# Dense heads of a two-layer encoder: the first half projection of a step ahead of the turned probabilities, and ScalarE's first exponential ahead of two copies

## The chip, the cores and the metric

The kernel runs on one core of one Trainium2 chip. The metric is the device time in microseconds (us); lower is better.

## The reference

The program is a trunk of two encoder layers over 16 meta tokens and 1024 real tokens, 1024 wide, in float32. Each layer projects the tokens, runs three groups of heads side by side (A: windowed attention, B: dense attention, C: a gated recurrence), projects back and normalises. The change touches group B only:

```python
def attend(q_blk):
    s = jnp.einsum('bqhcd,bkhcd->bhcqk', q_blk, k).astype(jnp.float32) * scale
    s = jnp.where(key_ok, s, NEG)
    p = jax.nn.softmax(s, axis=-1)
    a = p[:, :, 0] - lam * p[:, :, 1]
    return jnp.einsum('bhqk,bkhv->bqhv', a.astype(v.dtype), v)
```

There are four dense heads. Each has two components c of 64 wide queries and keys, and the two softmaxes are combined into one matrix `a`, which weighs values 128 wide. Queries and keys are rotated (RoPE) ahead of it, and the result is normalised and gated.

## The kernel before

The whole kernel is one hand-ordered program for five instruction streams: TensorE (PE), ScalarE (ACT), VectorE (DVE), GpSimd (POOL) and the DMA queue of SyncE. Each stream runs strictly through its own list and waits on semaphores. There is no planner at run time; the same Python lists are walked by every engine's builder, so that the counts agree.

**Tiles and steps.** Tokens lie in nine tiles (eight of 128 rows and one, the last, of 16 meta rows). Layer 0 needs all nine query tiles, layer 1 only the eight real ones. A *step* is one query tile t of one dense head g (B0 to B3). Steps run head by head, tile by tile. `b_step(l, g, t, k)` names the step k places further on.

**What a step does.** For step (g, t) the engines do the following, in `pass_b` of each engine.

- PE writes the scores of the *next* step (`scores`, L1116, 12 matmuls, two banks of PSUM per component: banks 2/3 and 4/5). It then waits for `b_comb`, DVE's combined probabilities `p0_b` of *this* step, and turns them by transposes in three groups of three tiles (`transposes(t, 0..2)`, L1272). Group 0 goes to bank 0, group 1 to bank 1, and group 2 to bank 0 again, so group 2 waits until ACT has copied group 0. Then come the products with the values (`values`, L1288, 18 matmuls with three copied groups as their input: tiles 0 to 5, then 6 to 8).
- DVE takes the maximum of the next step's scores for component 0 and for component 1 (`maximum`, L2131 and L2132, which writes `neg_max`), does low parts and rotations for the next head (`qk_lo` L2087, `qk_rope` L2073 to L2079), finishes the step before (`finish`, L2157 and L2160), and combines the next step's two exponentials (`combine`, L2141 to L2147; L2145 makes `p0_b` and raises `b_comb`).
- ACT copies the turned groups to `aT_b` (`evac_probs`, L1622), computes the next step's exponentials (`exps(after, c)`, L1610 and L1612; each waits for `b_max` of its component), copies the values (L1632) and computes the norm (L1639 to L1643).
- POOL splits weights into a high and a low part beside DVE's maxima (`beside_maximum`). SP moves rotated pieces, results and weights.

**ACT's order before**, in every step: copies of groups 0 and 1; the casts of a rotated piece if the step has one (`qk_hi_of`, L1585, for the pieces 0 and 1); the exponential of component 0; the copy of group 2; the cast of piece 2 if there is one; the exponential of component 1; `values_out`; `norm`.

**Projections inside the steps.** While one head attends, PE projects the queries and keys of the head behind it. Each projection (a feature half and a piece of 346 or 348 tokens, 24 matmuls, L944) is cut in two halves of 12 matmuls, and `b_steps(l, nx)` deals these halves out as `parts` of the steps. In layer 0 the heads B0, B1 and B2 have 2, 2, 1, 1, 1, 1, 1, 1, 2 halves, the same, and 2, 2, 2, 1, 1, 0, 0, 0, 0 over their nine steps. In layer 1 B0 and B1 have 2, 2, 2, 1, 1, 1, 1, 2 and B2 has 2, 2, 2, 2, 0, 0, 0, 0 over eight steps. B3 has none. In the very first step of B0 both halves are placed ahead of everything else on PE, and `parts` is emptied there. A projection of feature half f uses bank 7 - f. Before the change the first half of a step lies between the turned groups 1 and 2, the second between group 2 and the values.

**The last step of a head** also turns the next head's meta scores (`meta_turned` on PE, L1237 and L1241, in bank 6; `meta_out` on ACT, L1599 and L1600; `meta_bound` on DVE, which the next maximum needs). The projection in that step uses bank 6, too, and waits for `meta_out`.

The deal of halves, from `b_steps`:

```python
halves = [(nx, u, half) for u in units(l, nx, "qk") if u not in early(nx) for half in range(2)]
q, r = divmod(len(halves), n - 3 if after_next(nx) else n - 4)
ends = [(t + 1) * q + min(t + 1, r) for t in range(n)]
parts = [halves[a:b] for a, b in zip([0] + ends, ends)]
```

Of the kernel before, what the change touches and what calls it, by code (L numbers as in the profile page):

```python
# [63 lines left out]
def rows(t):  # L64
    return META if t == MT else P
# [422 lines left out]
def build(nc, x, meta, emb_ln_g, emb_ln_b, w_in, w_out, a_sink, b_lam, c_lb_logits, norm_cols,  # L488
# [3 lines left out]
    def sb(stack, name, shape, dt=F32):  # L492
        return stack.enter_context(nc.sbuf_tensor(name, shape, dt))
# [67 lines left out]
    qk = sb(sc, "qk", [P, 4, TOK])  # L561
# [115 lines left out]
    def slot_of(g):  # L677
        return (head_no(g) + 1) % 2
# [259 lines left out]
    def _(pe):  # L938
# [306 lines left out]
        def pass_b(l, g, nx):  # L1245
            def scores(step):
                if step is None:
                    return
                g, t = step
                sl = slot_of(g)  # L1250
                if t == 0:
                    pe.wait_ge(qk_lo_done, QK_PIECE[l, g, "qk", len(T_PIECES) - 1])
                m = rows(t)
                keys = [("s", l, g, t, c) for c in range(2)]
                for key in keys:
                    wait_free(pe, key)
                for i in range(2):
                    last = row_product(
                        lambda c: psum[0:m, bank(keys[c]) + i, :],
                        lambda a, c: qk_b[c * HD:(c + 1) * HD, sl, 2 * a, cols(t)],  # L1260
                        lambda b, c: qk_b[c * HD:(c + 1) * HD, sl, 2 * b + 1, i * 512:(i + 1) * 512])
                for key, ins in zip(keys, last):
                    ins.then_inc(filled[bank(key)], 1)

            def transposes(t, j):
                m = rows(t)
                key = ("aT", l, g, t, j)
                b = bank(key)
                wait_free(pe, key)
                for i in range(3):  # L1270
                    k = 3 * j + i
                    last = nc.tensor.transpose(psum[:, b, i * P:i * P + m],  # L1272
                                               p0_b[0:m, B_STEP[l, g, t] % 2, k * P:(k + 1) * P], ident[0:m, 0:m])
                last.then_inc(filled[b], 1)

            def values(t, ks=range(TILES)):
                m = rows(t)
                key = ("o", l, g, t)
                b = bank(key)
                if ks[0] == 0:  # L1280
                    if t == 0:
                        wait_read(pe, ("unit", l, g, "vg", TILES - 1))
                    wait_free(pe, key)
                for k in ks:
                    if k % 3 == 0:
                        wait_read(pe, ("aT", l, g, t, k // 3))

                    last = nc.tensor.matmul(psum[0:m, b, 0:P], aT_b[:, k, 0:m], vg_b[:, head_no(g), k, 0:P],  # L1288
                                            start=k == 0, stop=k == TILES - 1)
                if ks[-1] == TILES - 1:  # L1290
                    last.then_inc(filled[b], 1)

            if g == "B0":
                pe.wait_ge(b_pad, l + 1)
                scores((g, 0))
            for t, parts, _, _ in b_steps(l, nx):
                if (g, t) == ("B0", 0):

                    for h, x, half in parts:
                        project(l, h, "qk", x, half)  # L1300
                    parts = []
                scores(b_step(l, g, t, 1))
                if nx and t == q_tiles(l) - 1:
                    meta_turned(l, nx)
                pe.wait_ge(b_comb, B_STEP[l, g, t])
                transposes(t, 0)
                transposes(t, 1)
                if nx == B_HEADS[-1] and t == q_tiles(l) - 2:
                    meta_scores(l, nx)
                for h, x, half in parts[:1]:  # L1310
                    project(l, h, "qk", x, half)
                transposes(t, 2)
                for h, x, half in parts[1:2]:
                    project(l, h, "qk", x, half)
                values(t, range(6))
                if not nx and t >= Y_LAG:
                    transpose_y(l, t - Y_LAG)
                values(t, range(6, TILES))
                for h, x, half in parts[2:]:
                    project(l, h, "qk", x, half)  # L1320
                if after_next(nx) and t == q_tiles(l) - 2:
                    meta_scores(l, nx)
                for x in output_beside(nx, t):
                    project(l, "O", 0, x)
# [31 lines left out]
    def _(act):  # L1356
# [245 lines left out]
        def pass_b(l, g, nx):  # L1602
            def exps(step, c):
                g, t = step
                n = B_STEP[l, g, t]
                m, i = rows(t), n % 2
                act.wait_ge(b_max, B_COMP[l, g, t, c])
                b = bank(("s", l, g, t, c))
                probs = p0_b[0:m, i] if c == 0 else p1_b[0:m]
                nc.scalar.activation(probs[:, REAL * P:TOK], meta_s[0:m, slot_of(g), c, t, :], ACT.Exp, scale=SCALE,  # L1610
                                     bias=neg_max[0:m, i, c:c + 1], accum_out=row_sum[0:m, i, 2 * c + 1:2 * c + 2])
                nc.scalar.activation(probs[:, 0:REAL * P].rearrange("p (i n) -> p i n", i=2), psum[0:m, b:b + 2, :],  # L1612
                                     ACT.Exp, scale=SCALE, bias=neg_max[0:m, i, c:c + 1],
                                     accum_out=row_sum[0:m, i, 2 * c:2 * c + 1]).then_inc(released[b], 1)

            def evac_probs(t, j):
                key = ("aT", l, g, t, j)
                b, m = bank(key), rows(t)
                wait_filled(act, key)
                if b_step(l, g, t, -1) and j == 0:  # L1620
                    wait_filled(act, ("o", l, *b_step(l, g, t, -1)))
                nc.scalar.copy(aT_b[:, 3 * j:3 * j + 3, 0:m],  # L1622
                               psum[:, b, 0:3 * P].rearrange("p (k c) -> p k c", k=3)[:, :, 0:m])\
                    .then_inc(released[b], 1)

            def values_out(t):
                key = ("o", l, g, t)
                n, b = B_STEP[l, g, t], bank(key)
                wait_filled(act, key)
                if n > 2:  # L1630
                    act.wait_ge(b_y, n - 2)
                nc.scalar.copy(o_b[0:rows(t), n % 2, :], psum[0:rows(t), b, 0:P]).then_inc(released[b], 1)  # L1632

            def norm(step):
                g, t = step
                n, m = B_STEP[l, g, t], rows(t)
                wait_read(act, ("o", l, g, t))
                act.wait_ge(b_scale, n)
                then(nc.scalar.activation(b_junk[0:m, :], o_b[0:m, n % 2, :], ACT.Square,  # L1639
                                          accum_out=sumsq[0:m, t, 0:1]))  # L1640
                then(nc.scalar.activation(rstd[0:m, t, 0:1], sumsq[0:m, t, 0:1], ACT.Ln, bias=eps_rms[0:m],
                                          scale=fscale[0:m, n % 4, :]))
                nc.scalar.activation(rstd[0:m, t, 0:1], rstd[0:m, t, 0:1], ACT.Exp, scale=-0.5).then_inc(rstd_ready, 1)  # L1643

            if g == "B0":
                exps((g, 0), 0)
                exps((g, 0), 1)
            for t, _, _, before in b_steps(l, nx):
                after = b_step(l, g, t, 1)
                if nx and t == q_tiles(l) - 1:  # L1650
                    meta_out(l, nx)
                evac_probs(t, 0)
                evac_probs(t, 1)
                for j in before:
                    if j < len(T_PIECES) - 1:
                        qk_hi_of(l, nx, j)
                if after:
                    exps(after, 0)
                evac_probs(t, 2)
                for j in before:  # L1660
                    if j == len(T_PIECES) - 1:
                        qk_hi_of(l, nx, j)
                if after:
                    exps(after, 1)
                values_out(t)
                norm((g, t))
                if nx and t == q_tiles(l) - 2:
                    meta_rows_out(l, nx)
                if not nx and t >= Y_LAG:
                    hi_of_rows("y", l, t - Y_LAG)  # L1670
# [620 lines left out]
```

## Time and profile before

| | us |
|---|---|
| median of 3 runs | 1686.74 |
| lowest and highest | 1682.14, 1890.09 |
| the profiled execution | 1683.42 |
| its span | 1682.0 |
| layer 0, windows of heads B0, B1, B2 | 67.50, 72.50, 71.00 |

The profile is of one execution. The span is what its trace covers; the profiled execution's own time is 1.4 us more. In the rows, L944 is line 944 of the kernel. PE is TensorE's matmuls and PEld its weight loads. A row of a timeline gives the start in us from the start of the span, the length in us, the engine, the line, the operation with its output and inputs, the number of instructions merged into it (x12), and in brackets the idle time of the engine ahead of it with what released it. Instructions of one engine overlap in part, so times from start to start are better measures than the lengths.

### The profile page before, as it was taken

To read this page: it belongs to the slowest core of one execution; us is meant where nothing else is said; L and a number is where in the kernel's file an instruction comes from. 1 tells how busy PE (TensorE), PEld (TensorE's weight loads), DVE (VectorE), ACT (ScalarE), POOL (GpSimd) and SP (SyncE) were. 2 spreads that over 40 slices of the span, in tenths; PEclk is the share of its full clock that TensorE was granted. 3 is DMA by queue.
4 is the path that set the end of the run, shared out by engine and by line. 5 is a ranking of instruction groups with operands and counts; after the bars stand their busy time and mean duration, and the time that the engine had idled before them with its cause. 6 is when DMAs were issued, how large, how long until landed. Compare 5 with 4: busy or idle time off the path is not lost.

```text
span 1682.0 us, 38542 instructions
## 1 busy us (share of the span) xinstructions
PE 1564.1 (93%) x15296; PEld 1462.0 (87%) x15296; DVE 1072.4 (64%) x2421; ACT 874.8 (52%) x2569; POOL 408.2 (24%) x390
## 2 busy tenths in 40 slices
PE   3899999999999999789989999999999899987997
PEld 3899999999888888678989999999999789876897
DVE  7486684446557788775265866844555678787526
ACT  5444545356627676774045445452564477767504
POOL 5332321310121102020554413213103101112054
PEclk9999999999999999999999999999999999999999
DMA  7110201200120111143122102012002111114312
GB/s 280 52 52 14 65 27 37 80 30 11 39 85 17 50 26 50 37 141 109 51 76 90 52 14 65 27 36 79 30 11 72 53 26 51 51 27 146 107 65 101
DMA packets 97859, 102.32 MB, mean 61 GB/s; under 512 B 7504, under 2 KB 87744, under 8 KB 97424
## 3 DMA queue, kind: packets, MB, share of 16 engines
q1 hardware_dynamic: 96720, 98.78, 18.3%
q8 instruction: 123, 2.02, 0.5%
q10 hardware_dynamic: 960, 1.07, 0.2%
q14 instruction: 56, 0.46, 0.1%
HBM read 70.14 MB, written 21.17 MB: 54 GB/s over the span
## 4 chain that ended last, share of the span: by engine, by line
PE 59%; DVE 20%; ACT 11%; issue 4%; POOL 3%; DMA 3%; SPq 0%; ACTq 0%; DVEq 0%; POOLq 0%
PE psum L944 43%; PE psum L1288 3%; ACT p_b L1612 3%; PE psum L1272 3%; PE psum L1116 3%; DVE p_b L2145 3%; DVE row_max L2131 2%; DVE s_a L2001 2%; POOL w_lo L909 2%; ACT aT_b L1622 2%; PE psum L1013 2%; ACT pT_a L1528 1%; PE psum L991 1%; DMA qk_t<-rot 1%; ACT p_b L1610 1%
## 5 line engine op out<-in xcount | busy, mean ns | idle before, releaser
L944 PE MATMUL psum<-w_hi,hT_hi 128*128 128x256 f32 x1824 | 523.0, 287 | 9.5 <-POOL w_lo L909 8.2
L944 PE MATMUL psum<-w_hi,hT_lo 128*128 128x256 f32 x1824 | 513.1, 281 | 0.0
L944 PE MATMUL psum<-w_lo,hT_hi 128*128 128x256 f32 x1824 | 513.0, 281 | 0.0
L905 POOL CAST w_hi<-w_raw 128x512 fp32r<-128x512 f32 (+1 forms) x168 | 110.7, 659 | 1147.1 <-DMA w_raw<-in_w_in 685.9
L944 PEld LDWEIGHTS psum<-w_hi,hT_hi 128*128 128x128 f32 x1824 | 343.5, 188 | 18.3 <-POOL w_lo L909 10.1
L944 PEld LDWEIGHTS psum<-w_lo,hT_hi 128*128 128x128 f32 x1824 | 343.6, 188 | 0.0
L944 PEld LDWEIGHTS psum<-w_hi,hT_lo 128*128 128x128 f32 x1824 | 343.6, 188 | 0.0
L944 PE MATMUL psum<-hT_hi,w_hi 128*128 128x346 f32 (+1 forms) x672 | 226.0, 336 | 5.5 <-DVE hT_lo L1739 5.4
L909 POOL TENSOR_TENSOR w_lo<-w_raw,w_hi 128x512 fp32r<-128x512 f32 (+1 forms) x168 | 216.1, 1286 | 24.4 <-DVE neg_max L2132 12.5
L944 PE MATMUL psum<-hT_lo,w_hi 128*128 128x346 f32 (+1 forms) x672 | 217.8, 324 | 0.0
L944 PE MATMUL psum<-hT_hi,w_lo 128*128 128x346 f32 (+1 forms) x672 | 217.8, 324 | 0.0
L2131 DVE TENSOR_REDUCE row_max<-psum 128x1 f32<-128x1024 f32 x136 | 165.7, 1218 | 20.6 <-PE psum L1116 20.4
L1288 PE MATMUL psum<-vg_b,aT_b 128*128 128x128 f32 (+1 forms) x1224 | 155.4, 278 | 8.6 <-ACT aT_b L1622 8.4
L1288 PEld LDWEIGHTS psum<-vg_b,aT_b 128*128 128x128 f32 (+1 forms) x1224 | 142.6, 186 | 15.0 <-ACT aT_b L1622 11.8
L1612 ACT ACTIVATE p_b<-psum,neg_max 128x1024 f32<-128x1024 f32 x136 | 150.1, 1103 | 0.0
L944 PEld LDWEIGHTS psum<-hT_hi,w_hi 128*128 128x128 f32 x672 | 128.3, 191 | 7.9 <-issue 6.9
L1622 ACT COPY aT_b<-psum 128x384 f32<-128x384 f32 (+1 forms) x204 | 87.7, 463 | 88.2 <-PE psum L1272 87.0
L944 PEld LDWEIGHTS psum<-hT_hi,w_lo 128*128 128x128 f32 x672 | 128.5, 191 | 0.0
L944 PEld LDWEIGHTS psum<-hT_lo,w_hi 128*128 128x128 f32 x672 | 128.0, 191 | 0.0
L1116 PE MATMUL psum<-qk_b 64*128 64x512 f32 (+1 forms) x816 | 113.0, 408 | 13.7 <-ACT p_b L1612 13.2
L1272 PEld LDWEIGHTS psum<-ident,p_b 128*128 128x128 f32 (+1 forms) x612 | 67.2, 141 | 54.4 <-DVE p_b L2145 31.9
L1272 PE MATMUL psum<-ident,p_b 128*128 128x128 f32 (+1 forms) x612 | 92.9, 278 | 21.6 <-DVE p_b L2145 14.5
(179 smaller groups left out, 2372.8 us busy)
## 6 DMA issues: line engine op xcount, KB each, us to landing
w_raw<-in_w_in SPq DMA_DIRECT2D x72, 256.0 KB, 3.8
w_raw<-in_w_in SPq DMA_DIRECT2D x28, 512.0 KB, 4.4
h_dram<-hbuf SPq DMA_DIRECT2D x16, 512.0 KB, 2.9
w_raw<-in_w_out SPq DMA_DIRECT2D x16, 512.0 KB, 4.4
hbuf<-h_dram SPq DMA_DIRECT2D x16, 512.0 KB, 5.8
qk_b<-y_dram SPq DMA_DIRECT2D x16, 512.0 KB, 3.5
y_dram<-y_stage SPq DMA_DIRECT2D x96, 64.0 KB, 1.6
qk_t<-rot SPq DMA_DIRECT2D x56, 86.5 KB, 2.2
```

Source lines behind the costliest of these rows:

```text
L905: pool.tensor_copy(hi, raw).then_inc(w_hi_done, 1)
L909: pool.tensor_tensor(lo, raw, hi.bitcast(F32), ALU.subtract).then_inc(w_split, 1)
L944: last = nc.tensor.matmul(out_ap, lhs[a](k), rhs[b](k), start=k == 0 and a + b == 0, stop=k == KT - 1 and b == 1)
L1013: return nc.tensor.matmul(o_ap, k_sel[rs, k_at:k_at + H_ROWS], q_ap, start=True, stop=True)
L1116: last = [nc.tensor.matmul(out_of(r), q_of(a, r), k_of(b, r), start=i == 0, stop=i == 2) for r in range(2)]
L1272: last = nc.tensor.transpose(psum[:, b, i * P:i * P + m], p0_b[0:m, B_STEP[l, g, t] % 2, k * P:(k + 1) * P], ident[0:m, 0:m])
L1288: last = nc.tensor.matmul(psum[0:m, b, 0:P], aT_b[:, k, 0:m], vg_b[:, head_no(g), k, 0:P], start=k == 0, stop=k == TILES - 1)
L1612: nc.scalar.activation(probs[:, 0:REAL * P].rearrange("p (i n) -> p i n", i=2), psum[0:m, b:b + 2, :], ACT.Exp, scale=SCALE, bias=neg_max[ ...
L1622: nc.scalar.copy(aT_b[:, 3 * j:3 * j + 3, 0:m], psum[:, b, 0:3 * P].rearrange("p (k c) -> p k c", k=3)[:, :, 0:m])\
L2001: then(nc.vector.tensor_tensor_reduce(s_a[0:m, i, h, 0:w], psum[0:m, bank(key), 0:w], band_sb[0:m, band_columns(t)], 1.0, NEG, ALU.add, AL ...
L2131: then(nc.vector.tensor_reduce(row_max[0:m, i, c:c + 1], psum[0:m, b:b + 2, :], AX.XY, ALU.max))
L2145: stt(p0_b[0:m, i, 0:TOK], p1_b[0:m, :], coef[0:m, j, 0:1], p0_b[0:m, i, 0:TOK], ALU.mult, ALU.add).then_inc(b_comb, 1)
```

## The change

On PE, the first half projection of a step moves from between the turned groups 1 and 2 to ahead of the wait for `b_comb`, right behind the next step's scores (and behind `meta_turned` in a head's last step). The second half stays between group 2 and the values. On ACT, in the steps that have a half projection and a step behind them, the exponential of component 0 moves from behind the copies of groups 0 and 1 (and the casts behind them) to ahead of them. Steps without a half projection keep their order on both engines.

```diff
--- before.py
+++ after.py
@@ -1302,13 +1302,13 @@
                 scores(b_step(l, g, t, 1))
                 if nx and t == q_tiles(l) - 1:
                     meta_turned(l, nx)
+                for h, x, half in parts[:1]:
+                    project(l, h, "qk", x, half)
                 pe.wait_ge(b_comb, B_STEP[l, g, t])
                 transposes(t, 0)
                 transposes(t, 1)
                 if nx == B_HEADS[-1] and t == q_tiles(l) - 2:
                     meta_scores(l, nx)
-                for h, x, half in parts[:1]:
-                    project(l, h, "qk", x, half)
                 transposes(t, 2)
                 for h, x, half in parts[1:2]:
                     project(l, h, "qk", x, half)
@@ -1645,16 +1645,18 @@
             if g == "B0":
                 exps((g, 0), 0)
                 exps((g, 0), 1)
-            for t, _, _, before in b_steps(l, nx):
+            for t, parts, _, before in b_steps(l, nx):
                 after = b_step(l, g, t, 1)
                 if nx and t == q_tiles(l) - 1:
                     meta_out(l, nx)
+                if after and parts:
+                    exps(after, 0)
                 evac_probs(t, 0)
                 evac_probs(t, 1)
                 for j in before:
                     if j < len(T_PIECES) - 1:
                         qk_hi_of(l, nx, j)
-                if after:
+                if after and not parts:
                     exps(after, 0)
                 evac_probs(t, 2)
                 for j in before:
```

## Rows read from the trace of the kernel before

**Rows 1.** The page: busy time of each engine, and the chain by engine and line.

```profile
PE 1564.1 (93%) x15296; PEld 1462.0 (87%) x15296; DVE 1072.4 (64%) x2421; ACT 874.8 (52%) x2569; POOL 408.2 (24%) x390
...
PE 59%; DVE 20%; ACT 11%; issue 4%; POOL 3%; DMA 3%; SPq 0%; ACTq 0%; DVEq 0%; POOLq 0%
```

**Rows 2.** Windows: from-to, us, busy (instructions) of PE, PEld, DVE, ACT, POOL; clock; DMA share; GB/s.

```profile
559.40:631.90 72.50, 68.60 (x515) 60.12 (x514) 56.91 (x127) 50.75 (x152) 7.62 (x8) 1.00 0.14 38
```

**Rows 3.** Timeline of PE in one step with one half projection: start, length, group.

```profile
543.10 1.65 PE L1116 MATMUL psum<-qk_b 64*128 64x512 f32 x12
...
545.06 0.87 PE L1272 MATMUL psum<-ident,p_b 128*128 128x128 f32 x6 [0.32 <-DVE p_b L2145]
...
547.69 0.49 PE L1272 MATMUL psum<-ident,p_b 128*128 128x128 f32 x3
...
550.23 1.57 PE L1116 MATMUL psum<-qk_b 64*16 64x512 f32 x12
```

**Rows 4.** Timeline of ACT in the same step.

```profile
545.64 0.86 ACT L1622 COPY aT_b<-psum 128x384 f32<-128x384 f32 x2 [1.20 <-PE psum L1272]
...
546.44 0.31 ACT L1610 ACTIVATE p_b<-meta_s,neg_max 128x16 f32<-128x16 f32 x1
...
548.22 0.48 ACT L1622 COPY aT_b<-psum 128x384 f32<-128x384 f32 x1 [0.28 <-PE psum L1272]
...
548.59 0.31 ACT L1610 ACTIVATE p_b<-meta_s,neg_max 128x16 f32<-128x16 f32 x1
```

**Rows 5.** Timeline of DVE in the same step and at its end.

```profile
544.99 1.22 DVE L2131 TENSOR_REDUCE row_max<-psum 128x1 f32<-128x1024 f32 x1
...
550.19 0.16 DVE L2141 TENSOR_TENSOR inv_sum<-row_sum 128x2 f32<-128x2 f32 x1
...
552.13 1.21 DVE L2131 TENSOR_REDUCE row_max<-psum 16x1 f32<-16x1024 f32 x1
```

**Rows 6.** Timeline of PE in one step with two half projections.

```profile
569.00 1.65 PE L1116 MATMUL psum<-qk_b 64*128 64x512 f32 x12
...
570.58 0.87 PE L1272 MATMUL psum<-ident,p_b 128*128 128x128 f32 x6
...
573.19 0.49 PE L1272 MATMUL psum<-ident,p_b 128*128 128x128 f32 x3
...
577.52 1.65 PE L1116 MATMUL psum<-qk_b 64*128 64x512 f32 x12
```

**Rows 7.** Timelines of DVE and ACT in the same step.

```profile
570.68 1.23 DVE L2131 TENSOR_REDUCE row_max<-psum 128x1 f32<-128x1024 f32 x1 [0.91 <-PE psum L1116]
...
572.32 0.31 ACT L1610 ACTIVATE p_b<-meta_s,neg_max 128x16 f32<-128x16 f32 x1 [0.29 <-DVE neg_max L2132]
...
573.72 0.48 ACT L1622 COPY aT_b<-psum 128x384 f32<-128x384 f32 x1
```

**Rows 8.** Timeline of a step of the last head, which has no half projection.

```profile
721.56 0.87 PE L1272 MATMUL psum<-ident,p_b 128*128 128x128 f32 x6 [0.30 <-DVE p_b L2145]
...
722.14 0.86 ACT L1622 COPY aT_b<-psum 128x384 f32<-128x384 f32 x2 [1.45 <-PE psum L1272]
...
722.68 0.55 PE L1272 MATMUL psum<-ident,p_b 128*128 128x128 f32 x3 [0.24 <-ACT aT_b L1622]
```

**Rows 9.** Timelines of PE and ACT in a head's last step.

```profile
562.43 0.43 PE L944 MATMUL psum<-hT_hi,w_hi 128*128 128x348 f32 x1
...
564.54 0.35 PE L1272 MATMUL psum<-ident,p_b 16*128 16x16 f32 x3
...
566.07 0.18 ACT L1622 COPY aT_b<-psum 128x48 f32<-128x48 f32 x1
```

**Rows 10.** Timeline of ACT: the cast of a rotated piece.

```profile
588.97 0.79 ACT L1585 CAST qk_b<-qk_t 128x696 fp32r<-128x696 f32 x1
```

**Rows 11.** A long wait of PE, and the window behind it.

```profile
710.43 0.83 PE L1288 MATMUL psum<-vg_b,aT_b 128*16 128x128 f32 x6 [2.01 <-ACT aT_b L1622]
...
712.00:714.00 2.00, 2.00 (x12) 1.50 (x12) 1.79 (x5) 0.93 (x4) 0.00 (x0) 0.65 0.80 225
```

## Prediction, made before the changed kernel was run

> **What bounds the kernel now.** I read the page first, then the windows over the dense heads, then the timelines of three kinds of step. On the page the reader should see that TensorE is busy for 1564.1 us of a span of 1682.0 and carries 59% of the chain that ended last [rows 1]. So time is gained only where PE stands still, and lost wherever a new wait of PE appears. In the dense heads the window over head B1 of layer 0 shows PE busy for 68.60 of 72.50 us, at the full clock (1.00, the 2.4 GHz level) [rows 2]: about 4 us in nine steps to win there.
>
> A step with **one** half projection is a ring through three engines. Call C the moment at which DVE has combined the two probability matrices and goes on to the next maximum (544.99) [rows 5]. Then the first turned groups start on PE at C+0.07 (545.06), behind a wait of 0.32 for the combine, and the third group at C+2.70 (547.69), after the half projection [rows 3]. ACT copies that group at C+3.23 (548.22) and starts the second exponential at C+3.60 (548.59) [rows 4]. DVE reads its sum at C+5.20 (550.19) and is ready for the next maximum at C+7.14 (552.13), which is the next C [rows 5]. Scores to scores is 7.13 us (543.10 to 550.23) [rows 3]. ACT's first exponential starts at C+1.45 (546.44), released by DVE's negated maximum, and has room in front of the third copy, which sits idle for another 0.28 [rows 4].
>
> A step with **two** half projections takes 8.52 us (569.00 to 577.52), and PE has no wait in it [rows 6]; DVE waits for PE's scores, 0.91 us [rows 7]. There PE is the bound.
>
> **The steps that change.** From the planner's list: layer 0 has 22 steps, layer 1 has 19, in which a projection moves on PE (B0 without its first step, B1, and the first five or four steps of B2). Of these 41, 22 have one half and 19 have two; 4 of the 19 are a head's last step. ACT's order changes in the same 41 and in the first step of each layer's B0. No matmul, copy or DMA is added or removed: the cost is wholly one of waits. No queue of SP or POOL is reordered, and the banks of the moved half (6 and 7) are used by no turned group, so their order stays.
>
> **What is removed.** PE's wait for the combine ahead of the turned groups, 0.32 us in a single step [rows 3], none in a double one [rows 6]. From the scores' start to the turned groups' it takes 1.96 us in the single step (543.10 to 545.06) and 1.58 in the double one (569.00 to 570.58) [rows 3, 6], so at most 0.38 us is to be had 22 times: 8.4 us.
>
> **What is added, single step.** The half projection used to lie between groups 0/1 and group 2. It covered two things: ACT's copy of group 0, whose bank group 2 needs, and the first exponential. Now group 2 follows directly, and ACT has the exponential queued ahead of the copies. The exponential can't move up: it waits for the negated maximum, and DVE starts that maximum only at C. So it starts at C+1.45 as now [rows 4]. It holds ACT for 1.40 us (572.32 to 573.72) [rows 7], so copy 0 starts at C+2.85. Behind a copy, group 2 starts 0.54 us after the copy's start (722.14 to 722.68) [rows 8]: C+3.39, in place of C+2.70. From there the ring is the old one: copy 2 after 0.53, second exponential after 0.37, sum after 1.60, next maximum after 1.94 [rows 3 to 5]. The next C is 7.83 us after this one, against 7.14: **+0.69 us**. Is the projection itself late? PE's next scores start 2.54 us behind the third group [rows 3], at C+5.93; the scores take 1.58 to the next start and the half projection 2.11 (562.43 to 564.54) [rows 6, 9], so it is over at C+9.62, 1.8 us into the next ring, and with 0.58 from turning to copy (545.06 to 545.64) [rows 3, 4] the copies could start 2.4 us into it, ahead of the exponential's end at 2.85. So it is the exponential, not the projection, that decides. Queued behind it on ACT are all three copies, and PE stands at group 2 with group 2, the values and the next scores behind it.
>
> **Double step.** Count from the scores' start P. DVE's maximum starts at P+1.68 (570.68), ACT's exponential 1.45 later and copy 0 at P+4.53; group 2 follows at P+5.07. Today it starts at P+4.19 (573.19) [rows 6, 7]. PE has no wait to shrink there, so all of it counts: **+0.88 us** each. That holds for 15 double steps, and for the first single step behind each of the five runs of double ones, where PE is still the bound: 20 x 0.88 = 17.6 us. The other 17 single steps give 17 x 0.69 = 11.7 us.
>
> **A head's last step** computes the next head's scores, whose maximum is late because the meta scores come first. Now the third group starts at 564.54, with the half projection ahead of it from 562.43; the exponential ends only at 566.07, where a copy starts [rows 9]. Behind the change the two first copies start there, and group 2 between 0.3 (copies of 16 rows, layer 0) and 0.54 us later [rows 8]: at 566.4 to 566.6, or +1.8 to +2.1 us. The four steps cost 4 x 1.95 = 7.8 us. The moved half needs the bank that the meta scores leave; it starts at 562.43 in both orders, since it already waits there now [rows 9].
>
> **The two first steps of B0** get ACT's new order alone: +0.7 each as in a single step, 1.4 us. **The casts** (0.79 us, [rows 10]) of eleven of the reordered steps stood between the copies and the exponential and now stand behind both. They delay the third copy by about as much as before, but in one step (layer 0, B1, step 2) DVE has the cast's rest and a whole rotation to do behind it: some 1.6 us in all, my estimate.
>
> **Sum:** 17.6 + 11.7 + 7.8 + 1.4 + 1.6 = 40.1 us, on the profiled execution's 1683.4 (span 1682.0 and 1.4 around it): 1723.5, say **1724 us**. The median shown is 1686.74, 0.2% above the profiled execution, which lies nearer to the lowest run (1682.14); I forecast on the profiled one. No row of the kernel before shows this order of exponential and copies, so its cost has bounds on both sides: below, -8.4 us, if the copies were never late and only the waits went; above, 41 x 1.40 = 57 us, if every step paid a whole exponential. I take the ring's value because each link in it has a row.
>
> **Rivals.** *A. Only PE-bound steps pay.* If the single rings have more slack than I read, their 0.69 disappears and 28 us remain: 1712 us, within 2%. For it: DVE waits here and there. Against it: the links of the ring add up to 7.14 exactly, with no slack. *B. The clock gives way.* A wait of 2.01 us at 710.43 was followed by a window with a granted clock of 0.65, a mixture of the 1.2 and 2.4 GHz levels [rows 11]; the waits of the last steps grow to about 1.5 us. If the clock fell in each of the four, PE would lose up to half of some 4 us, 2 us each: +8, 1732 us. Against it: the 4 us that PE stands still in the nine steps of B1 leave that window at 1.00 [rows 2]. *C. Faster, on the other side.* If ACT takes the groups' copies in time, that is, if the exponential's 1.40 us were already over when group 0 is turned, only the combine wait goes: 1683.4 - 8.4 = 1675 us. It decides from the point at which the exponential starts before C+1.0 (group 0 is ready at C+2.4 in the new order); it starts at C+1.45 in the rows. *D. Nothing happens*, because the moved half only swaps one wait for another of equal length: 1683 us.
>
> The Trainium skill ("TensorE: Matmul & The Clock Gate", Part 4: PE-mode transpose) says that transposes do not count as PE activity in the way matmuls do. By that rule the new waits, which stand between turned groups, would look longer to the clock, and rival B would be likelier. The trace has turned groups beside waits in each single step and shows 1.00 in that window [rows 2], so I leave B small.
>
> **Chances.** The ring as worked out 0.77 (1724, own range 1712 to 1732, of which about 0.08 is below 2%), A 0.08, B 0.10, C 0.02, D 0.03. "Slower by over 2%" begins at about 1717 from the profiled execution; 2% is about what a measurement of this kernel can tell from no change. Slower: 0.69 + 0.10 = 0.79; same: 0.08 + 0.08 + 0.02 + 0.02 = 0.20; faster by over 2%: 0.01. The range 1706 to 1738 takes in A and B and leaves C and D out.
>
> **What would show it.** Right: in single steps PE waits about 1 us at the third group for ACT's copy, and scores to scores is 7.8; double steps take 9.4 us with a wait of 0.88 at the same place; last steps grow by about 2; the waits for the combine vanish from the steps with a half projection, and ACT's exponential starts 1.45 us behind each maximum with the copies right behind it. Wrong: if the third group starts less than 0.3 us behind the first two, or if the first exponential starts earlier than C+1.2, or if the steps of head B3, whose order is as before, change their length.

## The result, and the profile after

The changed kernel takes 1726.5 us (median of 4 runs, 1724.2 to 1728.4) against 1686.7 us for the kernel before (one of its four executions took 1890.1 us and is left out). The ratio on record is 1.0248, with a 95% interval of 1.0233 to 1.0262: slower. The two medians alone give 1.0236, which lies inside the interval. The forecast was 1724 us, slower, with a range of 1706 to 1738. The runs of before made later on other chips have medians of 1684.6 and 1683.5 us, so the difference in microseconds is nearer to 42 than to the 39.8 between the two medians. The spans of the two profiled executions say the same: 1724.3 less 1682.0 is 42.3 us.

The page of the changed kernel, busy time by engine and the chain by engine:

```profile
PE 1579.9 (92%) x15296; PEld 1467.2 (85%) x15296; DVE 1071.2 (62%) x2421; ACT 873.5 (51%) x2569; POOL 406.9 (24%) x390
...
PE 53%; DVE 22%; ACT 14%; issue 4%; POOL 3%; DMA 3%; SPq 0%; ACTq 0%; DVEq 0%; POOLq 0%
```

Beside [rows 1], PE's share of the chain fell from 59% to 53%, while DVE and ACT hold more of it. The number of instructions is the same. The window over head B1 of layer 0, with the columns of [rows 2]:

```profile
566.10:647.70 81.60, 70.83 (x515) 60.36 (x514) 56.87 (x127) 50.51 (x152) 7.53 (x8) 1.00 0.13 34
```

It was 72.50 us long and is 81.60, still at a clock of 1.00. PE's busy sum has grown a little, from 68.60 to 70.83, while the work is the same: a pipelined instruction that follows a wait shows a longer duration, and a busy sum doesn't tell work from such tails. Start-to-start times do.

What PE waited for (line waited at and releaser: us in total, times, longest), first in the kernel before,

```profile
PE psum L1272 <- DVE p_b L2145: 14.5, 35, 1.1
...
PE psum L1116 <- ACT p_b L1612: 13.2, 26, 1.2
...
PE psum L1288 <- ACT aT_b L1622: 8.4, 15, 2.0
...
PE psum L1272 <- ACT aT_b L1622: 5.3, 22, 0.2
```

then in the changed one:

```profile
PE psum L1272 <- ACT aT_b L1622: 44.8, 64, 2.4
...
PE psum L1116 <- ACT p_b L1612: 11.1, 22, 1.2
...
PE psum L1272 <- DVE p_b L2147: 7.3, 16, 1.0
...
PE psum L1288 <- ACT aT_b L1622: 6.4, 14, 1.4
```

These four lines show what the change did to PE's waits. The wait for the combined probabilities has halved, by 7.2 us. The wait for ACT's copies at the third turned group was 5.3 us in 22 short waits, and is 44.8 us in 64, up to 2.4 us long. The other two lines shrink by 2 us each. Together the four grew by 28.2 us, and PE's busy sum by 15.8 us, with the tails in it.

A step with one half projection on PE (scores, turned groups 0 and 1, group 2, the next scores):

```profile
548.37 1.65 PE L1116 MATMUL psum<-qk_b 64*128 64x512 f32 x12
...
551.97 0.81 PE L1272 MATMUL psum<-ident,p_b 128*128 128x128 f32 x6
...
553.62 0.55 PE L1272 MATMUL psum<-ident,p_b 128*128 128x128 f32 x3 [0.84 <-ACT aT_b L1622]
...
556.23 1.09 PE L1116 MATMUL psum<-qk_b 64*16 64x512 f32 x8
```

The wait of 0.32 us of [rows 3] is gone, and one of 0.84 us stands at the third group. Scores to scores is 7.86 us (548.37 to 556.23), where it was 7.13. The same step on DVE and ACT:

```profile
550.27 1.21 DVE L2133 TENSOR_REDUCE row_max<-psum 128x1 f32<-128x1024 f32 x1
...
551.71 0.31 ACT L1610 ACTIVATE p_b<-meta_s,neg_max 128x16 f32<-128x16 f32 x1 [1.90 <-DVE neg_max L2134]
...
553.11 0.84 ACT L1622 COPY aT_b<-psum 128x384 f32<-128x384 f32 x2
...
554.21 0.48 ACT L1622 COPY aT_b<-psum 128x384 f32<-128x384 f32 x1 [0.26 <-PE psum L1272]
...
554.58 0.31 ACT L1610 ACTIVATE p_b<-meta_s,neg_max 128x16 f32<-128x16 f32 x1
...
556.18 0.16 DVE L2143 TENSOR_TENSOR inv_sum<-row_sum 128x2 f32<-128x2 f32 x1 [0.64 <-ACT p_b L1612]
```

C, DVE's next maximum, is 550.27. The first exponential starts at C+1.44, as in [rows 4]; the two copies start right behind it at C+2.84, and the third group on PE 0.51 later, at C+3.35. The third copy is at C+3.94, the second exponential at C+4.31 and the sum at C+5.91. Forecast were 1.45, 2.85, 3.39, 3.92, 4.29 and 5.89. ACT is idle for 1.90 us ahead of the exponential, and the copies, for which PE stands, lie behind it.

A step with two halves, on PE:

```profile
586.88 1.65 PE L1116 MATMUL psum<-qk_b 64*128 64x512 f32 x12
...
590.46 0.82 PE L1272 MATMUL psum<-ident,p_b 128*128 128x128 f32 x6
...
591.93 0.55 PE L1272 MATMUL psum<-ident,p_b 128*128 128x128 f32 x3 [0.66 <-ACT aT_b L1622]
...
596.33 0.96 PE L1116 MATMUL psum<-qk_b 64*128 64x512 f32 x6
```

The step takes 9.45 us (586.88 to 596.33) against 8.52 in [rows 6], 0.93 us more. The third group starts 5.05 us behind the scores (586.88 to 591.93); before it was 4.19, and 5.07 was forecast. The trace calls 0.66 us of this a wait; it counts idle time only from the end of the instruction before.

A head's last step:

```profile
566.13 1.67 PE L1116 MATMUL psum<-qk_b 64*128 64x512 f32 x12
...
569.11 0.43 PE L944 MATMUL psum<-hT_hi,w_hi 128*128 128x348 f32 x1 [0.53 <-ACT meta_s L1600]
...
572.97 0.35 PE L1272 MATMUL psum<-ident,p_b 16*128 16x16 f32 x3 [1.22 <-ACT aT_b L1622]
...
577.43 0.95 PE L1116 MATMUL psum<-qk_b 64*128 64x512 f32 x5
```

The moved half still waits for the meta scores' copy (0.53) and then PE waits 1.22 us at the third group. The step takes 11.30 us (566.13 to 577.43), and took 9.55 (559.45 to 569.00 in the trace before).

Step by step over the whole trace, from one step's scores to the next (my sums of start times, by class of step; the column before the last is what the prediction gave):

| steps | number | before, us | after, us | forecast of the growth | growth |
|---|---|---|---|---|---|
| first step of B0 | 2 | 14.77 | 18.08 | 1.4 | 3.3 |
| two halves | 15 | 128.88 | 142.43 | 13.2 | 13.6 |
| one half | 22 | 166.07 | 184.43 | 17.7 | 18.4 |
| last step, two halves | 4 | 37.43 | 44.88 | 7.8 | 7.5 |
| no half projection | 21 | 164.80 | 164.75 | 0 | 0.0 |

The growths add up to 42.6 us, and the spans differ by 42.3: in sum, nothing outside these steps moved.

One row of the table is off, the first. In the first step of B0 PE has no half projection, so it waits at the third group for the exponential and the copy. On PE, and then a window with the columns of [rows 2]:

```profile
502.96 0.55 PE L1272 MATMUL psum<-ident,p_b 128*128 128x128 f32 x3 [2.41 <-ACT aT_b L1622]
...
503.38 3.32 PE L1288 MATMUL psum<-vg_b,aT_b 128*128 128x128 f32 x18
...
506.63 0.79 PE L1116 MATMUL psum<-qk_b 64*128 64x512 f32 x2
...
503.00:506.60 3.60, 3.60 (x21) 3.32 (x21) 1.55 (x5) 2.73 (x7) 0.00 (x0) 0.68 0.00 0
```

The wait is 2.41 us, and behind it the granted clock of the window is 0.68: part of it at the 1.2 GHz level. The values take 3.25 us to the next scores, where they take 2.10 in the double step ahead of the one above, at the full clock (584.78 to 586.88). The changed kernel was measured and profiled once more (see the experiments), and there the same step of layer 0 had no fall:

```profile
496.70 1.67 PE L1116 MATMUL psum<-qk_b 64*128 64x512 f32 x12 [0.59 <-ACT p_b L1612]
...
501.96 0.55 PE L1272 MATMUL psum<-ident,p_b 128*128 128x128 f32 x3 [2.42 <-ACT aT_b L1622]
...
504.87 1.65 PE L1116 MATMUL psum<-qk_b 64*128 64x512 f32 x12 [0.24 <-ACT p_b L1612]
```

With the same wait it takes 8.17 us (496.70 to 504.87), against 7.39 before and 8.94 with the fall. So the new order by itself costs 0.8 us in this step, and the rest of the row's 3.3 us goes with the clock.

One single step stands out as well, step 3 of head B1 in layer 0. It comes behind the step that has a cast and a whole rotation:

```profile
611.03 0.55 PE L1272 MATMUL psum<-ident,p_b 128*128 128x128 f32 x3 [2.33 <-ACT aT_b L1622]
```

It grew from 7.96 to 9.33 us. Its wait is nearly as long as that of the first step, and the window over it (604.30 to 613.63) shows a clock of 1.00.

### The profile page after: what moved, and what is told of

Same layout as the page of the kernel before. It is cut to its first block, busy times and chain, and to the rows that moved or that the text cites. A ratio compares the mean times of both kernels' runs of the same rounds, so it can differ in the third digit from the quotient of the medians.

```text
span 1724.3 us, 38542 instructions
## 1 busy us (share of the span) xinstructions
PE 1579.9 (92%) x15296; PEld 1467.2 (85%) x15296; DVE 1071.2 (62%) x2421; ACT 873.5 (51%) x2569; POOL 406.9 (24%) x390
## 3 DMA queue, kind: packets, MB, share of 16 engines
q1 hardware_dynamic: 96720, 98.78, 17.9%
## 4 chain that ended last, share of the span: by engine, by line
PE 53%; DVE 22%; ACT 14%; issue 4%; POOL 3%; DMA 3%; SPq 0%; ACTq 0%; DVEq 0%; POOLq 0%
PE psum L944 38%; ACT p_b L1612 5%; DVE row_max L2133 4%; PE psum L1288 3%; PE psum L1116 3%; DVE p_b L2147 3%; ACT aT_b L1622 2%; PE psum L1272 2%; DVE s_a L2003 2%; POOL w_lo L909 2%; PE psum L1013 1%; ACT p_b L1610 1%; ACT pT_a L1528 1%; PE psum L991 1%; DMA qk_t<-rot 1%
## 5 line engine op out<-in xcount | busy, mean ns | idle before, releaser
L2133 DVE TENSOR_REDUCE row_max<-psum 128x1 f32<-128x1024 f32 x136 | 165.6, 1218 | 28.5 <-PE psum L1116 28.3
L1288 PE MATMUL psum<-vg_b,aT_b 128*128 128x128 f32 (+1 forms) x1224 | 160.4, 283 | 6.4 <-ACT aT_b L1622 6.4
L1272 PE MATMUL psum<-ident,p_b 128*128 128x128 f32 (+1 forms) x612 | 92.5, 277 | 53.7 <-ACT aT_b L1622 44.8
```

The lines of the kernel that those rows point to most:

```text
L1272: last = nc.tensor.transpose(psum[:, b, i * P:i * P + m], p0_b[0:m, B_STEP[l, g, t] % 2, k * P:(k + 1) * P], ident[0:m, 0:m])
L2133: then(nc.vector.tensor_reduce(row_max[0:m, i, c:c + 1], psum[0:m, b:b + 2, :], AX.XY, ALU.max))
```

## The experiments

Each was run beside the kernel before on the same chip. "Ring theory" in the expectations is the chain worked out in the prediction.

**TensorE's part alone.** `parts[:1]` is projected ahead of `b_comb` as in the change; ScalarE as before.

```diff
+                for h, x, half in parts[:1]:
+                    project(l, h, "qk", x, half)
                 pe.wait_ge(b_comb, B_STEP[l, g, t])
...
-                for h, x, half in parts[:1]:
-                    project(l, h, "qk", x, half)
                 transposes(t, 2)
```

> TensorE's part of the change alone: the first half projection ahead of the turned groups, ScalarE's order as before. Ring theory (each step is a chain of DVE, ACT and PE whose longest path counts, so the two parts don't add): ACT copies groups 0 and 1 only when the projection is done, and the first exponential, the third copy and the second exponential queue behind them. Single steps grow to about 8.3 us, which is more than in the whole change (7.83); double steps grow only by about 0.5 (9.0). In all +40 us over before, 1723 to 1727, as much as the whole change. Rival (the parts add: each has its own share of the 40 us, because each puts its own wait on PE): about +20 us, 1705. Second rival (ScalarE's reordering alone does the harm): no more than +5 us.

Measured: 1721.0 us, ratio 1.0223 (1.0203 to 1.0244), +36 us by the medians (1684.6 before). Timelines of PE, then of DVE (the maximum at C), then of ACT, in a single step:

```profile
620.46 1.65 PE L1116 MATMUL psum<-qk_b 64*128 64x512 f32 x12 [0.55 <-ACT p_b L1612]
...
624.04 0.82 PE L1272 MATMUL psum<-ident,p_b 128*128 128x128 f32 x6
...
628.74 1.67 PE L1116 MATMUL psum<-qk_b 64*128 64x512 f32 x12 [0.55 <-ACT p_b L1612]
...
622.35 1.22 DVE L2131 TENSOR_REDUCE row_max<-psum 128x1 f32<-128x1024 f32 x1
...
624.57 0.86 ACT L1622 COPY aT_b<-psum 128x384 f32<-128x384 f32 x2 [3.02 <-PE psum L1272]
...
625.32 0.32 ACT L1610 ACTIVATE p_b<-meta_s,neg_max 128x16 f32<-128x16 f32 x1
...
627.07 0.34 ACT L1610 ACTIVATE p_b<-meta_s,neg_max 128x16 f32<-128x16 f32 x1
```

Here C is 622.35. PE starts groups 0 and 1 at C+1.69, because the projection lies ahead of them. ACT copies at C+2.22, which is past C+1.45, so the exponential comes behind the copies and starts at C+2.97. The second one starts at C+4.72, later than in the whole change (C+4.31). The step takes 8.28 us (620.46 to 628.74) against the 7.86 of the whole change. In the sums by class the single steps grew by 28.3 us, more than in the whole change (18.4), the double ones by 6.8 (13.6) and the last ones by 3.4 (7.5). Laid on top of this, ScalarE's reordering makes the single steps shorter and the double ones longer, as expected. The total by the medians is some 4 us below the 40 forecast, but the interval (34 to 41 us) takes 40 in, and the profiled execution is 39.8 us longer. Both rivals, +20 us and at most +5 us, are out.

**ScalarE's part alone.** The first exponential ahead of the copies in every step with `parts`; TensorE as before.

```diff
-            for t, _, _, before in b_steps(l, nx):
+            for t, parts, _, before in b_steps(l, nx):
...
+                ahead = bool(parts)
...
+                if after and ahead:
+                    exps(after, 0)
                 evac_probs(t, 0)
...
-                if after:
+                if after and not ahead:
                     exps(after, 0)
```

> ScalarE's part of the change alone: the first exponential ahead of the copies of groups 0 and 1 in the steps with a half projection, TensorE's order as before. Ring theory: the exponential starts 1.45 us behind the maximum in either case, so group 2 can be turned at C+3.39 whether the projection lies ahead of groups 0 and 1 or behind them; the time is that of the whole change to within 3 us, +40 to +43 (1724 to 1728), and single steps take 7.83 us. The wait of PE at group 2 is about 0.7 us in single steps, and the old wait of 0.3 us for the combine comes back. Rival (parts add): about +20 us. Second rival (TensorE's move alone does the harm): within 5 us of before.

Measured: 1727.4 us, ratio 1.0256 (1.0235 to 1.0277). That is the whole change's time again. Timelines of PE and ACT in a single step:

```profile
630.12 1.65 PE L1116 MATMUL psum<-qk_b 64*128 64x512 f32 x12
...
632.09 0.88 PE L1272 MATMUL psum<-ident,p_b 128*128 128x128 f32 x6 [0.32 <-DVE p_b L2148]
...
635.38 0.55 PE L1272 MATMUL psum<-ident,p_b 128*128 128x128 f32 x3 [0.50 <-ACT aT_b L1622]
...
637.98 1.33 PE L1116 MATMUL psum<-qk_b 64*16 64x512 f32 x10
...
633.47 0.31 ACT L1610 ACTIVATE p_b<-meta_s,neg_max 128x16 f32<-128x16 f32 x1 [1.90 <-DVE neg_max L2135]
...
634.86 0.85 ACT L1622 COPY aT_b<-psum 128x384 f32<-128x384 f32 x2
```

The groups 0 and 1 are turned at 632.09, behind the wait for the combine (0.32). But ACT doesn't copy them until 634.86, 2.77 us later, when the exponential is over. The third group waits 0.50 (0.7 was expected), and the step takes 7.86 us (630.12 to 637.98), like the changed kernel's. Double, single and last steps each sum to the changed kernel's within 0.5 us. So the position of the half projection makes no difference once ACT's exponential stands ahead of the copies. The two parts together cost 42 us, and each alone 36 and 43: they don't add, and both rivals fall: the one in which each part has its own share, and the one in which TensorE's move alone does the harm.

**Both parts, in single steps only.** The condition `len(parts) == 1` on both engines.

```diff
+                ahead = len(parts) == 1
+                if ahead:
+                    for h, x, half in parts[:1]:
+                        project(l, h, "qk", x, half)
                 pe.wait_ge(b_comb, B_STEP[l, g, t])
```

> Both parts of the change, but only in steps that have exactly one half projection; double steps, a head's last steps with two halves and the first step of a layer stay as before. Ring theory: 22 x 0.69 to 0.87 plus the casts, +18 us, 1702. Rival (only the PE-bound steps pay, single rings have slack): the double steps are as before, so +5 us or less, from the five first single steps.

Measured: 1702.7 us, ratio 1.0118 (1.0094 to 1.0141), +18.1 us by the medians. The single steps sum to 17.9 us more, and no other class changed by more than 0.1. Rival A of the prediction, that only the PE-bound steps pay, is out.

**Both parts, in double and last steps only.** The condition `len(parts) > 1`, and not in the first step of B0.

> The complement of the kernel with singles: both parts of the change only in the 19 steps with two half projections (15 inside a head, 4 last steps). Ring theory: 15 x 0.88 plus 4 x 1.95 us, +21 to +22 us (1705), and with the +18 of the singles the whole of the change (the classes of steps add, since each step hands on no slack). Rival (the last steps' clock falls, about 2 us each): +29 us.

Measured: 1707.0 us, ratio 1.0134 (1.0117 to 1.0152), +23.4 us by the medians, where +21 to +22 was expected; the interval (20 to 26 us) leaves out the rival's +29. The ratios' excesses of this kernel and the one before add to 0.0252, and the changed kernel measured beside this one has 0.0250 (1.0232 to 1.0268). In this profile one last step of layer 0 had a fall of the clock (see below), which made it 1.5 us longer.

**The double steps covered again.** As the kernel with double and last steps only, with the second half projection ahead of the third group too.

```diff
+                if ahead:
+                    for h, x, half in parts[1:2]:
+                        project(l, h, "qk", x, half)
                 transposes(t, 2)
-                for h, x, half in parts[1:2]:
+                for h, x, half in [] if ahead else parts[1:2]:
                     project(l, h, "qk", x, half)
```

> As the kernel with both parts in the double steps alone, with one edit more: the second half projection also stands ahead of group 2 (right behind groups 0 and 1), so that PE has 2 us of work while ACT is in the exponential and in the copy of group 0. Theory (what costs is that PE reaches group 2, whose bank waits for a copy queued behind the exponential, with nothing in between): the wait of 0.65 us and the 0.24 behind it vanish from the 15 double steps, and +4 to +7 us remain of +22, in the last steps and at heads' starts. Rival (it is the late exponentials and copies as such, whoever covers them): still +15 us or more.

Measured: 1692.7 us, ratio 1.0049 (1.0032 to 1.0066), +9.2 us by the medians: 14 of 23 us are back. That is more than the +4 to +7 expected (the interval is 5 to 11 us), and less than the rival's +15. A double step on PE:

```profile
577.45 1.65 PE L1116 MATMUL psum<-qk_b 64*128 64x512 f32 x12
...
583.58 0.49 PE L1272 MATMUL psum<-ident,p_b 128*128 128x128 f32 x3
...
586.12 1.65 PE L1116 MATMUL psum<-qk_b 64*128 64x512 f32 x12
```

There is no wait in it, with ACT's order still that of the change. It takes 8.67 us (577.45 to 586.12), 0.15 more than before, which was not in the expectation. By class the double steps grew by 1.6 us in all, the last steps by 2.4, and the single steps by 3.6. The single ones' growth lies in the five behind a double step, 3.9 us: PE waits there for the combine, 0.3 to 1.3 us, where it had no such wait before. So the lateness that PE doesn't pay in the double steps is partly paid one step later. The rest of the 9 us lies outside the steps, within what the runs of before differ by among themselves. Late copies thus put no wait on PE in the double steps, as long as PE has a projection between the groups that are copied and the group that needs their bank.

**The first step of B0 undone.** The changed kernel with ScalarE's old order in that step.

```diff
-                if after and parts:
+                ahead = parts and (g, t) != ("B0", 0)
+                if after and ahead:
                     exps(after, 0)
...
-                if after and not parts:
+                if after and not ahead:
                     exps(after, 0)
```

> The changed kernel with one thing undone: in the first step of head B0 of each layer ScalarE keeps its old order (TensorE has the same order there in both kernels). By the ring alone this step costs 0.7 to 0.8 us a layer, so this gains 1.5 us on the changed kernel. If the fall of the granted clock that the changed kernel's trace shows right behind that step's wait of 2.41 us is caused by that wait, the clock stays at 1.00 there and the gain is 4 us. Rival (the clock falls there for another reason): the fall remains and the gain is 1.5 us.

> The changed kernel again, unedited, on the same chip as the three above, as the base for the first step's kernel and for the sum of the classes: ratio to before 1.0248 by its first measurement, 1.023 to 1.026.

Measured: 1724.7 us, ratio 1.0241 (1.0221 to 1.0260), against 1726.1 us, ratio 1.0250 (1.0232 to 1.0268), for the changed kernel. The two intervals overlap, and the times don't decide between 1.5 and 4 us. The traces say more. With the old order the two first steps take 14.77 us again (in all), and the windows behind them show 1.00. None of the seven profiled executions with the old order (before, this kernel and five others) has a fall of the clock in or right behind a first step, 14 steps in all. With the new one, three profiled executions (the change twice, ScalarE's part alone once) have six such steps with a wait of 2.4 us, and in five of them the clock fell. So the fall there goes with the new order and its wait, and the rival in which it remains is out. But the profiled execution of the undone kernel had the fall elsewhere, in both last steps of layer 0. The changed kernel measured again had it in one of these; PE and the window behind it:

```profile
570.90 0.35 PE L1272 MATMUL psum<-ident,p_b 16*128 16x16 f32 x3 [1.23 <-ACT aT_b L1622]
...
574.05 2.94 PE L1288 MATMUL psum<-vg_b,aT_b 128*16 128x128 f32 x18
...
576.92 1.66 PE L1116 MATMUL psum<-qk_b 64*128 64x512 f32 x12
...
574.00:578.40 4.40, 4.40 (x31) 3.14 (x30) 1.01 (x2) 1.25 (x5) 0.00 (x0) 0.80 0.75 240
```

The 18 products with the values take 2.87 us to the next scores, where 2.07 is usual (575.36 to 577.43 in the trace of the change), and the step takes 12.85 instead of 11.30 us. Four profiled executions have such last steps with a wait of 1.2 us at the third group (the change twice, the doubles alone, the first step undone). The clock fell in 4 of their 8 last steps of layer 0, where the tile has 16 rows, and in none of the 8 of layer 1, where it has 128. ScalarE's part alone has one wait of 1.7 us there, and no fall in its 4 last steps. So in the last steps of layer 0 a fall differs from one execution of the same kernel to the next and is worth 1.5 us each time. Against the first profile of the change, the undone kernel's profile has 3.3 us less in the first steps and 3.1 us more in the last ones, from two such falls, so its total could not show the 4 us.

**The half projection of a single step in quarters.** From the kernel before, with an argument of `project` for the quarter: in single steps the half projection is cut again, one quarter between groups 1 and 2, the other between group 2 and the values. ScalarE as before.

```diff
+                single = len(parts) == 1
                 for h, x, half in parts[:1]:
-                    project(l, h, "qk", x, half)
+                    project(l, h, "qk", x, half, 0 if single else None)
                 transposes(t, 2)
+                if single:
+                    project(l, h, "qk", x, half, 1)
```

> Built on the kernel before, not on the change: in steps with one half projection, that half is split into two quarters of 6 matmuls, one between groups 1 and 2 as now, the other between group 2 and the values. ScalarE is as before. Ring theory: group 2 is turned 1 us earlier, ACT's copy of it then waits for the first exponential instead (its end at C+2.85), so the ring shortens by 0.37 us, from 7.14 to 6.77, where DVE has no full rotation (7.14 of DVE work) in the step; in all about -3 us (1680 to 1681 where before is 1683.5). Rival (single steps are bound by DVE's or PE's own work, not by the ring): no difference.

Measured: 1680.7 us (12 runs) against 1684.6, ratio 0.9982 (0.9973 to 0.9992). The single steps sum to 162.33 us, 3.7 less than before, and all other classes are the same within 0.2. It is faster than both kernels, by 0.2% against before. The gain is 3.9 us by the medians; the 3 us expected lie inside the interval, and the rival (no difference) outside it. The scores of two steps that follow each other, on PE, then ACT's third copy in the second:

```profile
606.04 1.65 PE L1118 MATMUL psum<-qk_b 64*128 64x512 f32 x12 [0.30 <-ACT p_b L1617]
...
613.05 1.65 PE L1118 MATMUL psum<-qk_b 64*128 64x512 f32 x12
...
617.59 0.46 ACT L1627 COPY aT_b<-psum 128x384 f32<-128x384 f32 x1
```

Scores to scores is 7.01 us (606.04 to 613.05), 7.12 before. The next step takes 6.76 us (613.05 to 619.81), where the same step took 7.14 before and 6.77 was expected. In it ACT's copy of the third group (617.59) comes right behind the exponential and no longer waits for PE. That was the slack of 0.28 us in [rows 4] turned to use, in the opposite direction to the change.

## Why the prediction was right

**The bound.** Both bounds were read rightly: a ring through DVE, PE and ACT without slack in single steps, PE in double ones. The singles-only kernel and the quarters show the ring, since a later third group lengthens a single step and an earlier one shortens it. The double steps covered again show the other bound: with PE busy in the same place, their growth is 1.6 us in place of 13.6.

**The single step's term.** The class was put at 17.7 us and grew by 18.4. In the step shown, the ring's links differ from the trace by 0.04 us at most. The parts of the class were not met as well as its sum. The 1.6 us for the casts was put on step 2 of head B1 in layer 0. That step and the one behind it grew by 2.3 us together, 0.8 more than their two ring terms. The other 20 steps grew by 1.4 us more in all than theirs. That the sum came out within 0.7 us is in part luck.

**The double step's term** was 0.88 and is 0.90 (9.50 less 8.59 on average). The text said that a wait of 0.88 us would show at the third group; the trace shows 0.66 and a third group that starts 0.86 us later. **The last steps** were put at 1.95 and took 1.86.

**What decides** was named as the exponential, not the projection, and ScalarE's part alone shows it: it costs as much as the whole, with the projection where it was. The prediction did not say that the projection's move alone costs almost as much by another way, since then the copies are late for want of turned groups, and the exponential behind them. That came with the expectation of that run. In the whole change the exponential is the later of the two, and the projection's lateness doesn't show behind it.

**The term that was mis-sized** is the first step of each layer: "+0.7 each as in a single step, 1.4 us" became 3.3. The ring's part of it was right, 0.8 us in the one such step without a fall of the clock. What the sum left out is that the granted clock falls behind that step's wait of 2.4 us, in five of six cases. Rival B looked for the clock in the last steps, not here.

**The rivals.** A fell with the singles-only kernel. C and D fell with the result. B, the clock, is true in kind and small in size. In the last steps it came in some executions, at 1.5 us each, and in none of the four in the first profile of the changed kernel, where B supposed 2 us in each. B rested on the wait of 2.01 us in [rows 11]. Six profiled executions have that wait with the clock at 1.00 up to its end (before, the singles, the quarters, the doubles, the doubles covered again, the first step undone); the clock fell behind it in four and stayed at 1.00 in the last two. The rule of the Trainium skill ("TensorE: Matmul & The Clock Gate", Part 4: PE-mode transpose) that transposes do not count as activity spoke for it. The falls did come where a wait stands next to turned groups. But the wait of 2.33 us in step 3 of head B1 stands between turned groups too, and the clock stayed at 1.00. Turned groups with no wait, as in most double steps of the kernel before, left it at 1.00 as well. No run varies the turned groups beside one and the same wait, so none shows what the transposes add.

**What the change was worth** in its own terms: the wait for the combine shrank by 7.2 us. The upper bound given for it was 8.4.

## What to carry to other kernels

A wait that a piece of work seems to cause may be what that piece hides: before moving it, list every dependence that matures beside it (here a bank's copy), and ask who covers that in the new place. On an engine whose list is worked through in order, a long instruction whose input is not there yet must not stand ahead of a short one that another engine waits for. Where a step is a ring through several engines, add up its links from one timeline; if they make the step's length exactly, a shift of a link shows up in full (0.69 us forecast, 0.73 in the step shown), and the parts of a change need not add (36 and 43 us alone, 42 together).

## What the runs showed of the hardware that was not expected

The granted clock can fall behind a single wait of PE, and the length of the wait alone doesn't decide it.

- First steps of B0 in the new order, with a wait of 2.4 us: it fell in 5 of 6. From third group to third group it is 8.17 us without the fall (501.96 to 510.13, the changed kernel measured again) and 8.93 to 10.38 with it, so a fall cost 0.8 to 2.2 us. Both layers have the same two steps there, but the one case without a fall is of layer 0.
- Step 3 of head B1 in layer 0, with a wait of 2.33 us: it stayed at 1.00 in all four profiled executions that have this wait (the change twice, the singles, the first step undone). There PE has a half projection between the scores and the turned groups. In the first step it has none, and waits of 0.59 and 0.33 us stand ahead of the long one. Whether that makes the difference is not shown.
- Last steps, with a wait of 1.2 us: it fell in 4 of 8 where the tile has 16 rows, at 1.5 us each, and in none of 8 where it has 128.
- In the other steps with a half projection of the changed kernel, waits of 0.6 to 1.1 us, one to a step, left it at 1.00.
- At the border of heads B2 and B3 in layer 0, whose order the change leaves alone, it fell in 8 of the 10 profiled executions, the kernel before included [rows 11]. In four of them it was low before the long wait there began (in the changed kernel from 729.6 us, with the wait ending at 732.5).
